# A bidirectional encoder layer on one core: first loads reordered and split between two queues, spare TensorE products ahead of loads and scores, rotary tables scaled on another engine

## The reference

```python
shift1, scale1, gate1, shift2, scale2, gate2 = silu(c) @ w_ada + b_ada      # w_ada (1024, 6144)
h = rms_norm(x) * (1 + scale1) + shift1
qa, ka, va, qb, kb, vb, ga, gb = split(h @ w_in)                            # w_in (1024, 3584)
qa = axial_rope(rms_norm(qa, q_norm_g)) * 64 ** -0.5                        # 8 heads of 64, 2 key heads
ka = axial_rope(rms_norm(ka, k_norm_g))
oa = softmax(qa @ ka.T) @ va @ w_branch_a                                   # global attention
ob = window_attention(qb, kb, vb, rel_bias, sink) @ w_branch_b              # |i-j| <= 128, relative bias
x = x + gate1 * ((sigmoid(ga) * oa + sigmoid(gb) * ob) @ w_out)
h2 = rms_norm(x) * (1 + scale2) + shift2
x = x + gate2 * expert_choice_moe(h2)                                       # 16 experts, width 2048
y = rms_norm(x, norm_f_g)
```

## Time and profile before

| | us |
|---|---|
| median of 3 runs | 2347.8 |
| lowest, highest | 2345.27, 2349.53 |
| the profiled execution, device time | 2345.38 |
| its span, first to last instruction | 2343.5 |
| TensorE busy | 2264.1 (97%) |
| chain that ended last, on PE | 89% |
| mean granted TensorE clock | 0.989 of full |

### The profile page before, as it was taken

One profiled execution on the slowest core, in us unless ns is written; L12 is line 12 of the kernel. 1 busy time (PEld: TensorE's weight loads), 2 busy tenths in 40 slices (PEclk: granted clock), 3 DMA queues, 4 the chain that ended last, 5 costly groups with the idle time before them and its releaser, 6 DMA issues.

```text
span 2343.5 us, 54934 instructions
## 1 busy us (share of the span) xinstructions
PE 2264.1 (97%) x23867; PEld 1663.0 (71%) x23974; DVE 1624.1 (69%) x1989; ACT 1218.1 (52%) x1552; POOL 1101.3 (47%) x711
## 2 busy tenths in 40 slices
PE   8998999999999999878999999999999999999996
PEld 3554676664444458678888888888888888888874
DVE  4776666582222456767787888788878878887875
ACT  4323665593111236445666566655655655666654
POOL 0000111132333215656666677666767767766742
PEclk9999999999999999989999999999999999999998
DMA  9102201403222445667899999989998999999896
GB/s 341 41 19 72 55 2 44 174 2 90 54 54 63 122 140 163 212 234 279 309 326 346 311 340 331 325 317 340 332 318 326 344 320 316 341 332 323 320 326 244
DMA packets 252439, 524.24 MB, mean 224 GB/s; under 512 B 8411, under 2 KB 57676, under 8 KB 252076
## 3 DMA queue, kind: packets, MB, share of 16 engines
q1 hardware_dynamic: 241692, 488.51, 59.2%
q0 software_dynamic: 10512, 32.25, 4.7%
HBM read 492.42 MB, written 28.31 MB: 222 GB/s over the span
## 4 chain that ended last, share of the span: by engine, by line
PE 89%; DVE 3%; DMA 2%; ACT 2%; POOL 2%; issue 2%; SPq 1%; DVEq 0%; POOLq 0%; ACTq 0%
PE ps L1824 24%; PE ps L1825 24%; PE ps L1823 23%; PE ps L2206 4%; PE ps L1999 3%; PE ps L2011 3%; PE ps L1876 3%; PE ps L2145 1%; PE ps L1911 1%; ACT arena L1082 1%; DMA arena<-w_in 1%; PE ps L1852 1%; PE ps L2172 1%; PE ps L1949 1%; PE ps L1901 1%
## 5 line engine op out<-in xcount | busy, mean ns | idle before, releaser
L1824 PE MATMUL ps<-arena 128*128 128x160 bf16 (+4 forms) x5617 | 1392.2, 267 | 9.0 <-issue 3.2
L1825 PE MATMUL ps<-arena 128*128 128x160 bf16 (+4 forms) x5620 | 1393.1, 267 | 0.4
L1823 PE MATMUL ps<-arena 128*128 128x160 bf16 (+4 forms) x5528 | 1359.0, 265 | 5.4 <-POOL arena L855 5.1
L1653 DVE TENSOR_TENSOR arena<-arena 128x2048 bf16<-128x2048 f32 x379 | 912.1, 2411 | 211.2 <-ACT arena L969 208.9
L969 ACT ACTIVATE arena<-arena 128x2048 bf16<-128x2048 f32 x384 | 726.3, 1904 | 218.8 <-PE ps L1825 175.9
L1823 PEld LDWEIGHTS ps<-arena 128*128 128x128 bf16 x5624 | 551.2, 98 | 156.7 <-issue 17.2
L1825 PEld LDWEIGHTS ps<-arena 128*128 128x128 bf16 x5624 | 551.1, 98 | 152.3
L1824 PEld LDWEIGHTS ps<-arena 128*128 128x128 bf16 x5624 | 551.1, 98 | 143.3 <-issue 2.9
L865 POOL TENSOR_TENSOR arena<-arena 128x320 bf16<-128x320 f32 x128 | 256.6, 2005 | 10.0
L862 POOL TENSOR_TENSOR arena<-arena,ones 128x320 bf16<-128x320 f32 x128 | 194.1, 1516 | 136.5 <-DVE arena L1702 136.2
L1219 ACT ACTIVATE arena<-ps 128x160 f32<-128x160 f32 x256 | 77.7, 303 | 313.0 <-PE ps L1825 313.0
(11 more groups left out here) (259 smaller groups left out, 2209.8 us busy)
## 6 DMA issues: line engine op xcount, KB each, us to landing
arena<-w_e_gate SPq DMA_DIRECT2D x64, 2048.0 KB, 9.0
arena<-w_e_up SPq DMA_DIRECT2D x64, 2048.0 KB, 9.8
arena<-w_e_down SPq DMA_DIRECT2D x64, 2048.0 KB, 9.1
arena<-w_ada SPq DMA_DIRECT2D x12, 2048.0 KB, 9.2
arena<-w_in SPq DMA_DIRECT2D x30, 512.0 KB, 5.3
arena<-x_sample SPq DMA_DIRECT2D x16, 512.0 KB, 3.7
arena<-w_in SPq DMA_DIRECT2D x3, 2048.0 KB, 16.5
arena<-w_out SPq DMA_DIRECT2D x2, 2048.0 KB, 9.1
```

The lines of the kernel that those rows point to most:

```text
L1653: ve.tensor_tensor(lo, stage_half(kind, a), hi, ALU.subtract).then_inc(lo_done, 1)
L1823: pe.matmul(out, w_hi, x_hi, start=start, stop=False)
L1824: pe.matmul(out, w_hi, x_lo, start=False, stop=False)
L1825: return pe.matmul(out, w_lo, x_hi, start=False, stop=stop)
```

## The change

- SP issues `w_ada` chunks 0 and 1 first, then token tile 0, chunk 2, tile 1, chunk 3. The seven small loads (`vec` in five pieces, `relc`, `oneh`) are issued by ACT's queue, ahead of its steps.
- On SP the second chunk of `w_in` goes ahead of the gains and tables, token tile 2 ahead of the store of `brow`, and the three router loads behind the token tiles.
- Step order: four `br` stay ahead of `AR 0`, the other four go between the `AR` steps; `XP 0` and `XP 1` move behind `AC 0` and `AC 1`.
- `keep_warm(out, n)` is new. It issues n bf16 products of 128 rows, 128x128 weights and 256 columns of the identity's bits, into a bank that the next step overwrites. There are 12 ahead of `vec`, 5, 4, 4, 4 ahead of `br 0` to `br 3`, 8, 12, 10, 10 ahead of `AR 0` to `AR 3`, and 4, 4, 28 ahead of `S 0`, `S 1`, `S 2`.
- `tab` goes from DVE to POOL: one instruction on the gains, two of 512 and four of 256 elements a partition. DVE waits for them (`tab_ready`) in `N 0`.

```diff
@@ plan_steps
-    s = [("vec",)] + [("br", h) for h in range(8)]
-    s += [("XP", 0), ("XP", 1), ("AR", 0), ("AR", 1), ("AC", 0), ("AR", 2), ("AC", 1), ("AR", 3), ("AC", 2),
-          ("AC", 3), ("A1",), ("X", 0), ("X", 1), ("HL", 1), ("HL", 0), ("WQ", 0), ("WQ", 1), ("tab",), ("WQ", 2), ("XP", 2)]
+    s = [("vec",), ("br", 0), ("br", 1), ("br", 2), ("br", 3), ("AR", 0), ("br", 4), ("AR", 1), ("AC", 0), ("XP", 0),
+         ("br", 5), ("AR", 2), ("AC", 1), ("XP", 1), ("br", 6), ("br", 7), ("AR", 3), ("AC", 2), ("AC", 3), ("A1",),
+         ("X", 0), ("X", 1), ("HL", 1), ("HL", 0), ("WQ", 0), ("tab",), ("WQ", 1), ("WQ", 2), ("XP", 2)]
@@ block.sync
-            for r, n, src in rows:
-                sp.dma_start(vec[r:r + n, :], src).then_inc(small_in, 16)
-            sp.dma_start(relc[:], rel_bias).then_inc(small_in, 16)
-            sp.dma_start(oneh, onehot).then_inc(small_in, 16)
+            for c in range(2):
+                mod_load(c)
             for t in range(2):
                 sp.dma_start(xt[:, t], token_rows(x_d, t)).then_inc(x_in[t], 16)
-            for c in range(4):
-                sp.dma_start(at(ada_slot[c], KD, 512), ada_v[:, :, c * 512:(c + 1) * 512]).then_inc(ada_in[c], 16)
+                mod_load(2 + t)
             sp.wait_ge(t_done, job_at[(("AR", 0), 0)] + 1)
             sp.dma_start(wqkv[0], win_v[:, :, 0:512]).then_inc(win_in[0], 16)
+            w_in_load(1)
...
-            for c in range(1, 3):
-                sp.wait_ge(t_done, job_at[(("AR", c), 0)] + 1)
-                sp.dma_start(wqkv[c], win_v[:, :, c * 512:(c + 1) * 512]).then_inc(win_in[c], 16)
-            for k in range(3):
...
+            w_in_load(2)
...
+            x_load(2)
             sp.wait_ge(brow_ready, 8)
...
@@ block.gpsimd
+                if k == "tab":
+                    gp.wait_ge(table_in, 16 * 7)
+                    gp.tensor_scalar(gains[:, 0], gains[:, 0], HD ** -0.5, None, ALU.mult).then_inc(gain_ready, 1)
+                    gp.wait_ge(gain_ready, 1)
+                    for n in range(2):
...
@@ block.scalar
+            for r, n, src in rows:
+                ac.dma_start(vec[r:r + n, :], src).then_inc(small_in, 16)
+            ac.dma_start(relc[:], rel_bias).then_inc(small_in, 16)
+            ac.dma_start(oneh, onehot).then_inc(small_in, 16)
@@ block.vector
                 if k in ("N", "NC"):
+                    if t == 0:
+                        ve.wait_ge(tab_ready, 6)
@@ block.tensor
+            def keep_warm(out, n):
+
+                half = ident[:].bitcast(BF16)
+                for _ in range(n):
+                    pe.matmul(out[:, 0:2 * P], half[:, 0:P], half, start=True, stop=True)
+
                 if k == "vec":
-                    pe.wait_ge(small_in, 16 * 7)
                     pe.wait_ge(const, 5)
                     b = bank(s)
+                    keep_warm(b, 12)
+                    pe.wait_ge(small_in, 16 * 7)
...
                 if k == "br":
+                    b = bank(s)
+                    keep_warm(b, (5, 4, 4, 4, 0, 0, 0, 0)[s[1]])
...
                 if k == "AR":
...
+                    if c < 4:
+                        keep_warm(b, (8, 12, 10, 10)[c])
...
                     if narrow(i):
+                        if i <= 2:
+                            keep_warm(ps[:, bank_of(job_at[(("T", 0, 0), 0)])], (4, 4, 28)[i])
                         if i >= 2:
                             pe.wait_ge(e_done, 2 * i - 2)
```

More of the change, by code:

```diff
@@ L407, in encoder @@
         const = sem("const")
-        relb_ready = sem("relb_ready")
+        relb_ready, gain_ready, tab_ready = sem("relb_ready"), sem("gain_ready"), sem("tab_ready")
         z_done = sem("z_done")
@@ L610, in mw_load, with x_load @@
                                      wbr_v[b][v][:, :, m * P:(m + 1) * P]).then_inc(mw_in[k % 2], 16)
+            def x_load(t):
+                sp.wait_ge(xn_ready, t - 1)
+                sp.dma_start(xt[:, t % 2], token_rows(x_d, t)).then_inc(x_in[t % 2], 16)
+            x_load(2)
             sp.wait_ge(brow_ready, 8)
@@ L614, in _ @@
                          brow.rearrange("p h r -> p (h r)")).then_inc(bias_out, 16)
-            for t in range(2, NT):
-                sp.wait_ge(xn_ready, t - 1)
-                sp.dma_start(xt[:, t % 2], token_rows(x_d, t)).then_inc(x_in[t % 2], 16)
+            for t in range(3, NT):
+                x_load(t)
+            for k in range(3):
+                a, b = [(0, 3), (3, 6), (6, 8)][k]
+                sp.dma_start(wr[:, a:b, :], w_router[0].rearrange("(k p) e -> p k e", p=P)[:, a:b, :])\
+                    .then_inc(wr_in, 16)
             sp.wait_ge(g_done, 3 * NT)
@@ L766, in _ @@
                 k = s[0]
+                if k == "tab":
[3 more added lines that the diff above has]
+                    for n in range(2):
+                        cos = tabs[:, 2 * n]
+                        gp.tensor_tensor(cos, cos, gains[:, n].unsqueeze(1).to_broadcast([P, 8, HD]), ALU.mult)\
+                            .then_inc(tab_ready, 1)
+                        for a in range(2):
+                            sin = tabs[:, 2 * n + 1].rearrange("p x (u a v) -> p x u a v", u=2, a=2)[:, :, :, a]
+                            g_ = gains[:, n].rearrange("p (u a v) -> p u a v", u=2, a=2)[:, :, 1 - a]
+                            gp.tensor_tensor(sin, sin, g_.unsqueeze(1).to_broadcast([P, 8, 2, 16]), ALU.mult)\
+                                .then_inc(tab_ready, 1)
                 if k == "RB":
@@ L981, in split_tail @@
                 split_high(kind, slot, h % 2, 64 * NE - (32 if kind == 2 else 16) + 16 * (h // 6) + 16)
+            rows = [(0, 8, c_p[0].rearrange("(r p) -> r p", p=P)), (8, 8, c_s[0].rearrange("(r p) -> r p", p=P)),
+                    (16, 48, b_ada[0].rearrange("(r p) -> r p", p=P)),
+                    (64, 8, n1g[0].rearrange("(r p) -> r p", p=P)), (72, 8, n2g[0].rearrange("(r p) -> r p", p=P))]
+            for r, n, src in rows:
+                ac.dma_start(vec[r:r + n, :], src).then_inc(small_in, 16)
+            ac.dma_start(relc[:], rel_bias).then_inc(small_in, 16)
+            ac.dma_start(oneh, onehot).then_inc(small_in, 16)
             for s in steps:
@@ L1380, in _ @@
                     mod_affine(A2, 72, 32)
-                if k == "tab":
-                    ve.wait_ge(table_in, 16 * 7)
-                    for n in range(2):
-                        for x in range(8):
-                            tc_, ts_ = tabs[:, 2 * n, x], tabs[:, 2 * n + 1, x]
-                            ve.tensor_tensor(tc_, tc_, gains[:, n], ALU.mult)
-                            for a in range(2):
-                                ins = ve.tensor_tensor(
-                                    ts_.rearrange("p (u a v) -> p u a v", u=2, a=2)[:, :, a],
-                                    ts_.rearrange("p (u a v) -> p u a v", u=2, a=2)[:, :, a],
-                                    gains[:, n].rearrange("p (u a v) -> p u a v", u=2, a=2)[:, :, 1 - a], ALU.mult)
-                    link(ins)
-                    link(ve.tensor_scalar(tabs[:, 0:2], tabs[:, 0:2], HD ** -0.5, None, ALU.mult))
                 if k == "XP":
```

12 lines of the change are left out of this document (5 added, 7 removed).

## The result

The changed kernel takes **2350.5 us** (median of 20 runs, 2346.8 to 2352.6), the kernel before 2346.4 beside it (20 runs, 2343.6 to 2349.5): ratio 1.0016, 95% interval 1.0010 to 1.0023. The profiled execution took 2350.80 with a span of 2349.0, against 2345.38 and 2343.5.

A forecast was written before the change was run, and what follows sets the result against it. PE bounds the kernel, so gains come only where it waits or runs slowly: the start (-4.0) and first scores (-1.2), from 2345.4 to 2340.2 profiled; 2342.6 us for the median, range 2338.6 to 2347.8.

The forecast's parts named there:

- Small loads ... I put them at 5.6: At the start, the small loads, which landed before 5.05 in the kernel before, were put at 5.6 us.
- The rival: Late small loads: slowed beside the large stream (POOL stores 5.7 us against 3.0), nothing gained from 6.8 on; chance 0.09.
- At full clock: ...: PE's start steps from vec to the last br, spare products included, run at full clock, AR 0 done by 14.5.
- the 27.0 of the sum: At the start, PE's steps ahead of AR 3 end at 27.0, 1.1 us to spare before w_ada's last chunk at 28.1.
- 40 spare products cost nothing while the loads are awaited; without that cover they would cost 4.3.: At the start, 40 spare products hide behind the wait for loads; uncovered they would cost 4.3 us.
- Transfers: At the start, last w_ada chunk lands at 28.1 (2.2 us earlier), third w_in chunk at 50.6; G 0 gains 4.0 us.
- The 7.35 us from `AR 3` to `G 0`: At the start, unchanged PE, ACT and DVE work of 7.35 us before G 0, which then starts at 35.5.
- Scores, -1.2: At the first scores, 28 spare products hold the clock and S 3's maximum gains 1.2 us, bounds 0.8 and 1.7.
- What DVE gains stays: Behind the first scores, DVE has no more gaps until 232, so the 1.2 us gain is kept.
- tab and SP's order, "nothing": At the start, tab on POOL is done by 51, wanted near 62; SP's new queue order also changes nothing.
- Half clock: Rival at the start: clock stays at half until AR 0, G 0 ends at 61.8, run takes 2346.6; chance 0.20.
- memory-rate rule: For the start's loads, a 358 GB/s limit would add 3.6 us and leave a gain of 0.4; chance 0.03.

The follow-up runs named there:

- a1: The changed kernel with the seven small loads issued by SP ahead of the first w_ada chunk: 2344.0 us, ratio 0.9986 to the kernel before.
- b3: The changed kernel with SP's first w_ada issue held back until ACT's seven small loads have landed: 2345.0 us, ratio 0.9994 to the kernel before.
- a4: The changed kernel with 48 spare products ahead of vec instead of 12: 2343.3 us, ratio 0.9987 to the kernel before.
- b2: The changed kernel with 48 spare products ahead of vec and none ahead of br and AR: 2339.0 us, ratio 0.9978 to the kernel before.
- c1: The kernel before with tab moved from DVE to POOL alone: 2346.1 us, ratio 0.9998 to the kernel before.
- c2: The kernel before with the second w_in chunk issued ahead of gains and tables, nothing else: 2343.7 us, ratio 0.9994 to the kernel before.
- a2: The changed kernel without the 69 spare products of the start, those at the scores kept: 2341.6 us, ratio 0.9979 to the kernel before.
- c3: The changed kernel with four small loads on SP, three on ACT, and spare products at vec, AR 2, AR 3 changed: 2344.5 us, ratio 0.9996.

## Why the prediction was wrong

The first split product was forecast at 57.6 and came at 67.6. `AR 3` started at 39.5 and not at 28.1, 11.4 us late; the rest made up 1.4 of it, since the third chunk of `w_in` no longer held it up.

- **"Small loads ... I put them at 5.6": the step that failed first.** They came at 8.69, 3.1 later. The 5.6 came from a quiet stretch, and now a full stream ran beside them; held apart from it they come at 5.0 (a1, b3). The rival had a row for it: 2.7 us more between large loads. Added to 5.05 that is 7.8, far nearer to 8.69; the sum should have gone by that row.
- **"At full clock: ..."** failed next. The pause grew to 3.98 us and the granted clock fell at its end; with the pause filled it stayed up (a4). From `vec` to the end of `br 3` it took 12.3 us (8.69 to 20.97) and not 6.1, from there to the end of `AR 0` 5.1 and not 2.8. Of the 12.5 us by which `AR 3` came behind the 27.0 of the sum, 3.1 are the loads, 8.5 these two stretches at half clock, 1.0 the remaining steps (with rounding).
- **"40 spare products cost nothing while the loads are awaited; without that cover they would cost 4.3."** The condition did not hold. Taking them out, with the 17 ahead of `br`, gave 3.1 us at `G 0` (a4 to b2), net of b2's own stretches at half clock and of the wait of `AR 3` for its load.
- **Transfers.** Right: last `w_ada` chunk at 27.8 (forecast 28.1). The third chunk of `w_in` was issued only at 35.8: SP waited for `AR 1` until 30.5 and then issued the second chunk, gains and tables until 35.8. It landed 16 us later, harmless as `G 0` reached it at 61. The 7.35 us from `AR 3` to `G 0` held to the digit.
- **Scores, -1.2.** Right in size (-1.10) at the maximum of `S 3`. "What DVE gains stays" failed: by the wide maximum the clock had taken it back, here and in four more of ten executions.
- **tab and SP's order, "nothing".** c1's median agrees for `tab` alone, though its start was 2.7 late for a reason left open. With `w_in` earlier and `tab` still on DVE, DVE is the next bound (c2), which the sum did not see.
- **The rivals.** Half clock and late loads were each described rightly and weighed as alternatives. In this kernel they are one event: late loads make the pause, and the pause costs the clock (a4 without it). The pause is not the only way to lose it: b3 had its loads in time and fell to half at 8.1. Together by their own prices, `G 0` ends at 61.8 + 3.1 = 64.9; less 61.6 and 1.2 that is +2.1, a median of 2349.9. Measured: 2350.5. That this is so near is luck: `G 0` ended at 67.6 and not 64.9, and the 2347.8 it starts from lay 1.4 above the median of 20 runs. The 0.07 for slower came of keeping the two apart.
- **Small slips.** The small loads are 0.11 MB and not 0.15. The 3.6 us of the memory-rate rule come to 3.3 by its own figures. By its own prices the late-load rival breaks even at 6.6 and not 6.8. None of them changes the forecast by more than 0.1 us.

## What to carry to other kernels

Small loads that everything waits for land late beside a full stream, also from a queue of their own: the second queue saves 2.6 us of issue time here and pays 3.6 in landing time. Whether to send them first depends on what the chain behind them costs: b2 and a2 have them late and are no slower than a1, b3 and c3, which have them in time; small loads first and no spare products behind them was not tried. Spare products were worth their time in the pause ahead of the wait for those loads, and cost more than they gave behind it, where TensorE was the bound. Change one thing at a time: one load moved in SP's list (c2) gives the whole gain that b2 has at the first split product. And when two rivals share a cause, price them together.

## What the runs showed of the hardware

- Seven loads of 0.11 MB on a second queue: the last one landed within 1.9 us of its issue with the other queue idle (b3), 5.5 us beside a full stream (changed; 372 GB/s from 5 to 8).
- A PE without a pause is not always one at full clock. Bias products ran for 14 us back to back at half clock in the kernel before; among 48 spare products the pace doubled on the way (6.73 us for all in a4, 2.74 for 12 alone in the changed kernel); in c3 the clock fell at 28.8 with no pause of PE before.
- A fall of the clock that is prevented can come later: the spare products ahead of `S 2` kept the clock through the first scores in all ten executions that have them, and in five it fell later instead, between 231 and 242.
- POOL and DVE slow each other in these traces: POOL's product of 128x256 in f32 took 0.7 us in the changed kernel at 48.4 and 49.1, 1.7 at 51.0 and 52.7 beside DVE's TENSOR_TENSORs there, and 2.8 beside the halvings of c1; these took 3.0 each (6.09 for two) instead of 2.2. No variant isolates it.
